# Projection weights stored partition by partition, cache copies cut into 8 KB pieces and partly placed later

## The chip, the cores and the metric

One Trainium2 chip, one of its cores. The metric is the device time of one launch in microseconds (us), lower is better.

## What is computed

One inference step of a one-layer decoder, for a prompt of 1024 tokens and for 8 sample sequences of 4 new tokens (1056 token rows, D = 1024), all float32. Cut to what matters here:

```python
q_a, k_a, v_a, u_b, q_c = split(x @ w_in)            # w_in is 1024 x 2048
attn = mix_of_dilated_windows(q_a, k_a, v_a)          # (128,1), (512,4), (2048,16)
pool = multi_pool(u_b); km, vm = split(mem @ w_mem_kv)
memo = mem_attention(q_c, km, vm)
h1 = layer_norm(alpha * x + concat(attn, pool, memo) @ w_o)
y  = layer_norm(alpha * h1 + hier_moe(h1))            # 32 experts
# for the samples, the K/V windows of 2048 rows move on by the 4 new rows:
new_win_k = concat(cache_win_k, k_new)[:, 4:]         # 8 sequences x 2048 rows x 512
new_win_v = concat(cache_win_v, v_new)[:, 4:]
```

The last two lines are pure copying: 2044 of 2048 rows (2 KB each) of 8 sequences, for K and V, go from the input to the output in HBM. That is 67 MB read and 67 MB written, and nothing in the kernel depends on it.

## The kernel before, in words

The stages come one after another: projection, attention (48 units, with the samples' attention worked in between), output projection with the first layer norm and the router ("mix"), 32 experts, second layer norm. Each engine has a program of its own, written out by hand, and semaphores between them.

**Projection.** The 1056 columns of x transposed (`xT`) and the weights lie in SBUF. Each is split into a rounded high part (ACT, L352, through `rounded_part`) and the rest (DVE, L358, through `rest`), and TensorE adds three products. The list `proj` holds 49 output tiles in the order q (tiles 0 to 11, weight block 0), k (12 to 23, block 1), v (24 to 32, block 2), q_c and u (33 to 44, block 3), memory K/V (45 to 48). A weight block is `[128, 8, 512]`, 2 MB, and has two places, `WF[0]` and `WF[1]`. Blocks 0 and 1 are issued by SP at the start; blocks 2 and 3, `w_mem_kv` and `memT` are issued by POOL (L1565 to L1570), each when `proj_done` says that the tiles using its place are evacuated. Tile n goes to PSUM bank n % 8. DVE evacuates the even tiles (L1134), ACT the odd ones (L962). `splits_after` puts the splits of block 2 behind the evacuations of tiles 12 to 19, and those of block 3 behind tiles 24 to 31: a split that waits for its weights holds up all evacuations behind it on ACT and DVE, and with them TensorE, which can be at most eight tiles ahead.

**The copies.** `copies` has 32 entries of 1022 rows (2,093,056 bytes), numbered 0 to 31 here, issued by SP (L521) in `copy_cache`, which waits for the copy two before it: two are in flight. SP issues 24 (`COPIES_FIRST`) during the projection, and then the score tables (L436), the sample biases and the first two ring loads.

**Attention.** The samples' cached keys and values come through a ring of two slots (L536, from `winkT`, `cache_win_v` and so on); load n may be issued only when step n-2 has been executed by TensorE (`s_xp`). SP issues loads 0 and 1, then all small outputs, then the last 8 copies, and only then load 2. PE's sample steps are `x_step`; those named "ss" use `winkT`.

**Mix.** For each chunk c of 128 rows SP loads `x` (L581, two buffers) and stores `h1` three chunks later (L576).

Of the kernel before, what the change touches and what calls it, by code (L numbers as in the profile page):

```python
# [22 lines left out]
P = 128  # L23
D = 1024
KT = D // P
SEQ = 1024
DB, DT = 8, 4
# [6 lines left out]
N_MEM = 256  # L34
WB = 2048
PB = 15
# [15 lines left out]
NVT = NK // P  # L52

ARENA = 51984
COPIES_FIRST = 24

CAP = 112
LN_SPLIT = 128
# [56 lines left out]
def build(nc, I, O):  # L115
    ctx = ExitStack()
    with ctx:
# [55 lines left out]
        XF, WF = at(18576, KT, TOK), [at(35472 + 8192 * s, KT, 512) for s in range(2)]  # L173
        MT = at(39568, KT, N_MEM)
# [60 lines left out]
        s_xk = [sem(f"s_xk{k}") for k in range(KT)]  # L235
        s_w = [sem(f"s_w{g}") for g in range(5)]
        s_mem, s_state = sem("s_mem"), sem("s_state")
# [46 lines left out]
        def rows(c):  # L284
            return P if c < CH - 1 else SMP
# [214 lines left out]
        @block.sync  # L500
        def _(sp):
            xv = I["xT"].rearrange("(k p) n -> p k n", p=P)
            wv = I["w_in"].rearrange("(k p) n -> p k n", p=P)
            for k in range(KT):
                sp.dma_start(XF[:, k, :], xv[:, k, :]).then_inc(s_xk[k], 16)
                sp.dma_start(WF[0][:, k, :], wv[:, k, 0:512]).then_inc(s_xk[k], 16)
                if k == 1:
                    sp.dma_start(CS[:, :], I["c_small"]).then_inc(s_const, 16)
            sp.dma_start(WF[1], wv[:, :, 512:1024]).then_inc(s_w[1], 16)
            sp.dma_start(USF[:, :, 0:PB], I["stateT"]).then_inc(s_state, 16)  # L510
            sp.dma_start(WPL2[:, :, :], I["w_pool"].rearrange("(m h) c e -> (h c) m e", h=2)).then_inc(s_state, 16)
            sp.dma_start(PSC, I["pool_scale"]).then_inc(s_state, 16)
# [4 lines left out]
            def copy_cache(n):  # L517
                t, b, r = copies[n]
                if n >= 2:
                    sp.wait_ge(s_copy[n % 2], 16 * (n // 2))  # L520
                sp.dma_start(O["win_" + t + "_s"][b, r * half:(r + 1) * half, :],  # L521
                             I["cache_win_" + t][b, DT + r * half:DT + (r + 1) * half, :]).then_inc(s_copy[n % 2], 16)

            for n in range(COPIES_FIRST):
                copy_cache(n)
            load_table(sp, 0)
            sp.dma_start(SBIAS, I["c_sample"]).then_inc(s_bias, 16)
# [1 line left out]
            for n, e in enumerate(ring_user):  # L529
                if n == 0:  # L530
                    proj_done(sp, n_x - 1)
                if n >= 2:
                    sp.wait_ge(s_xp, xnum[ring_user[n - 2]] + 1)
                dst, srcs = ring_load(n, e)
                for d, s in zip(dst, srcs):
                    sp.dma_start(d, s).then_inc(s_ring[n % 2], 16)  # L536
                if n == 1:
                    load_table(sp, 1)
                if n == 2:
                    load_table(sp, 2)  # L540
                if n == 7:
                    load_table(sp, 3)
                if n == 1:
                    proj_done(sp, NPROJ - 1)
                    sp.dma_start(O["kT"].rearrange("(m p) n -> p m n", p=P), KTT[:, :, 0:SEQ]).then_inc(s_store, 16)
                    sp.dma_start(O["v"].rearrange("(c p) n -> p c n", p=P), V[:, 0:CH - 1, :]).then_inc(s_store, 16)
                    sp.dma_start(O["kmT"].rearrange("(m p) n -> p m n", p=P), KM).then_inc(s_store, 16)  # L547
                    sp.dma_start(O["vm"].rearrange("(m p) n -> p m n", p=P), VM).then_inc(s_store, 16)
                    sp.dma_start(O["uT"].rearrange("(m p) n -> p m n", p=P), UP[:, :, UH + SEQ - PB:UH + SEQ]).then_inc(s_store, 16)
                    sp.wait_ge(s_state, 48)  # L550
                    sp.dma_start(O["poolT_s"], USF[:, :, DT:DT + PB]).then_inc(s_store, 16)
                    for b in range(DB):
                        sp.dma_start(O["win_v_s"][b, WB - DT:WB, :], V[DT * b:DT * b + DT, CH - 1, :]).then_inc(s_store, 16)  # L553
                    sp.wait_ge(s_xe, xnum[("knew",)] + 1)
                    for b in range(DB):
                        sp.dma_start(O["win_k_s"][b, WB - DT:WB, :], KN[DT * b:DT * b + DT, :]).then_inc(s_store, 16)
                    for c in range(COPIES_FIRST, len(copies)):
                        copy_cache(c)

            wo = I["w_o"].rearrange("(k p) n -> p k n", p=P)  # L560
# [17 lines left out]
            for c in range(CH):  # L578
                if c >= 2:
                    sp.wait_ge(s_r, c - 1)  # L580
                sp.dma_start(XR[c % 2][0:rows(c), :], I["x"][c * P:c * P + rows(c), :]).then_inc(s_x[c % 2], 16)  # L581
                if c >= 3:
                    store_h1(c - 3)
            sp.wait_ge(s_mix, CH)
# [974 lines left out]
        def _(pool):  # L1559
            step = Steps(pool, s_pl)  # L1560
            G = nc.gpsimd

            wv = I["w_in"].rearrange("(k p) n -> p k n", p=P)
            proj_done(pool, last_of[0])
            G.dma_start(WF[0], wv[:, :, 1024:1536]).then_inc(s_w[2], 16)  # L1565
            proj_done(pool, last_of[1])
            G.dma_start(WF[1], wv[:, :, 1536:2048]).then_inc(s_w[3], 16)
            proj_done(pool, last_of[2])
            G.dma_start(WF[0], I["w_mem_kv"].rearrange("(k p) n -> p k n", p=P)).then_inc(s_w[4], 16)
            G.dma_start(MT, I["memT"].rearrange("(k p) n -> p k n", p=P)).then_inc(s_mem, 16)  # L1570

            proj_done(pool, n_x - 1)
            pool.wait_ge(s_state, 48)
# [105 lines left out]
def laid_out(i):  # L1679

    a = {n: np.asarray(v) for n, v in i.items()}
    x = np.concatenate([a["x_prompt"].reshape(SEQ, D), a["x_sample"].reshape(SMP, D)])

    wk = a["cache_win_k"][0][:, ROWS].reshape(2, 4, 4, KC, 4, 2, HD)
    wk = wk.transpose(0, 3 - 1, 5, 6, 4, 1, 3).reshape(8, P, 4, 4 * KC)
    mk = a["cache_mem_k"][0].reshape(DB, N_MEM, 2, 2, HD).transpose(3, 4, 2, 0, 1).reshape(P, 2, DB * N_MEM)
    out = {
        "x": x, "xT": x.T, "memT": a["mem_prompt"][0].T, "stateT": a["state_pool"][0].transpose(2, 0, 1).reshape(2, P, DB, PB).transpose(1, 0, 2, 3).reshape(P, 2 * DB, PB),
        "winkT": wk, "memkT": mk,
        "cache_win_k": a["cache_win_k"].reshape(DB, WB, D_A), "cache_win_v": a["cache_win_v"].reshape(DB, WB, D_A),  # L1690
        "cache_mem_v": a["cache_mem_v"].reshape(DB, N_MEM, D_C),
        "w_in": a["w_in"][0], "w_mem_kv": a["w_mem_kv"][0], "w_pool": a["w_pool"][0], "pool_scale": a["pool_scale"][0].reshape(2, P).T,
        "w_o": a["w_o"][0], "w_r": np.concatenate([a["w_r1"][0], a["w_r2"][0].transpose(1, 0, 2).reshape(D, NE)], axis=1),
        "b_r": np.concatenate([a["b_r1"][0], a["b_r2"][0].reshape(NE)]),
        "w_gate": a["w_gate"].reshape(NE, D, DE), "w_up": a["w_up"].reshape(NE, D, DE), "w_down": a["w_down"].reshape(NE, DE, D),
        **{n: a[n][0] for n in ("ln1_g", "ln1_b", "ln2_g", "ln2_b")}, **shape_constants(),
    }
    return {n: np.ascontiguousarray(v) for n, v in out.items()}
# [24 lines left out]
```

## Time and profile before

| | |
|---|---|
| median of 3 runs | 1153.97 us |
| the runs | 1158.05, 1153.97, 1153.77 us |
| span of the profiled execution | 1155.0 us |
| that span less the median | 1.0 us |
| TensorE matmul busy | 935.7 us, 81% |
| DVE, ACT, POOL busy | 372.0, 261.9, 196.7 us |
| DMA queue 1 (issued by SP) | 247.97 MB |
| DMA queue 0 (issued by POOL) | 24.66 MB |
| time to landing of a cache copy, median | 13.3 us (K), 13.0 us (V) |
| chain that ended last | PE 64%, DMA 10%, DVE 10%, unknown queue 6% |

The span is what the profile's page covers, and every time below is counted from its start. The profile gives no other time of that execution; the span is 1.0 us above the median. A matmul busy share is not a share of TensorE's peak. The chain of waits is followed back from the last instruction; what it calls an "unknown queue" is a wait whose end no record explains. Of a DMA, "time to landing" runs from its issue to its completion, so it contains the time behind other transfers.

### The profile page before, as it was taken

The numbers are of one execution on the slowest core, as the hardware profiler recorded it, in microseconds if no ns is written. First come the engines' busy times: TensorE is split into PE (matmuls) and PEld (weight loads), VectorE is DVE, ScalarE is ACT, GpSimd is POOL, SyncE is SP. The second block draws the span as 40 slices with busy tenths as digits, with TensorE's granted clock in tenths as the row PEclk, the third lists the DMA queues.
The fourth block names the chain that finished last, engine by engine and source line by source line (L and its number), as shares of the span: only waits on it lengthen the run. The fifth ranks groups of instructions, "written<-read, shape, count | busy, mean of one in ns | idle before, by whom it ended". The sixth has DMA issues, their size and how long they took to land.

```text
span 1155.0 us, 16340 instructions
## 1 busy us (share of the span) xinstructions
PE 935.7 (81%) x6468; PEld 734.8 (64%) x6468; DVE 372.0 (32%) x788; ACT 261.9 (23%) x553; POOL 196.7 (17%) x260
## 2 busy tenths in 40 slices
PE   6993199996868999988999539999999999999100
PEld 6992187993545555557887338878787877878000
DVE  5200202006643556483544460010010101010496
ACT  5100101002433344382222101111111111111121
POOL 0000000042111222250000001212121212211276
PEclk9997599998988999998999758999999999999655
DMA  8999995338997747513221776999898999981461
GB/s 312 340 344 325 342 350 186 110 143 246 306 319 305 252 153 257 186 67 98 74 84 49 261 235 202 326 307 323 291 315 297 324 309 331 313 294 34 173 227 59
DMA packets 118458, 273.43 MB, mean 237 GB/s; under 512 B 13984, under 2 KB 82080, under 8 KB 116224
## 3 DMA queue, kind: packets, MB, share of 16 engines
q1 hardware_dynamic: 108352, 247.97, 63.2%
q0 software_dynamic: 10048, 24.66, 6.2%
q8 instruction: 40, 0.66, 0.2%
q14 instruction: 18, 0.15, 0.0%
HBM read 256.33 MB, written 95.30 MB: 304 GB/s over the span
## 4 chain that ended last, share of the span: by engine, by line
PE 64%; DMA 10%; DVE 10%; another core or an unknown queue 6%; issue 3%; SPq 3%; ACT 2%; POOL 1%; POOLq 0%; DVEq 0%; ACTq 0%
PE psum L641 60%; DMA back<-w_in 4%; DMA out_win_v_s<-cache_win_v 4%; PE psum L700 2%; DVE middle L1221 1%; DMA back<-winkT 1%; DVE front L1456 1%; ACT front L1078 1%; DVE stats L1547 1%; SPq L553 1%; DVE middle L1544 1%; DVE middle L1543 1%; POOL back L1600 1%; SPq L547 1%
## 5 line engine op out<-in xcount | busy, mean ns | idle before, releaser
L641 PE MATMUL psum<-back,front 128*64 128x128 f32 (+2 forms) x1280 | 149.6, 302 | 11.5 <-DVE back L490 7.9
L641 PE MATMUL psum<-x_high,w_high 128*128 128x352 f32 x288 | 95.2, 330 | 54.5 <-DVE w_low L358 54.3
L641 PEld LDWEIGHTS psum<-back,front 128*64 128x64 f32 (+2 forms) x1280 | 108.5, 164 | 45.8 <-issue 30.7
L641 PE MATMUL psum<-back 128*128 128x112 f32 (+3 forms) x1152 | 124.0, 311 | 12.9 <-DMA back<-winkT 10.7
L641 PE MATMUL psum<-front 64*128 64x512 f32 (+5 forms) x448 | 122.1, 514 | 12.1 <-DVE stats L1190 7.4
L641 PEld LDWEIGHTS psum<-back 128*128 128x128 f32 (+1 forms) x1152 | 112.2, 170 | 25.3 <-issue 19.0
L641 PE MATMUL psum<-back,middle 128*128 128x112 f32 (+1 forms) x880 | 101.8, 316 | 1.7 <-issue 1.7
L641 PEld LDWEIGHTS psum<-back,middle 128*128 128x128 f32 (+1 forms) x880 | 91.3, 181 | 14.5 <-issue 14.5
L641 PEld LDWEIGHTS psum<-front 64*128 64x128 f32 (+2 forms) x448 | 52.1, 194 | 67.1 <-issue 48.9
L641 PE MATMUL psum<-x_low,w_high 128*128 128x352 f32 x288 | 94.1, 327 | 0.0
L641 PE MATMUL psum<-x_high,w_low 128*128 128x352 f32 x288 | 94.0, 326 | 0.0
L1600 POOL TENSOR_SCALAR back<-consts,stats 128x128 f32<-128x128 f32 x96 | 57.4, 610 | 199.7 <-DVE stats L1203 141.3
L641 PEld LDWEIGHTS psum<-x_high,w_high 128*128 128x128 f32 x288 | 55.5, 193 | 55.2 <-DVE w_low L358 55.2
L1456 DVE TENSOR_TENSOR front<-front,psum 128x224 f32<-128x224 f32 x32 | 12.4, 388 | 225.5 <-ACT front L1078 225.5
L1461 DVE TENSOR_SCALAR front<-psum,back 112x512 f32<-112x512 f32 x32 | 24.0, 751 | 126.4 <-PE psum L641 126.4
L1620 POOL COPY back<-back 128x1 uint32 (+1 forms) x64 | 12.1, 188 | 303.3 <-DVE front L1461 258.7
L641 PE MATMUL psum<-wo_high,cat_high 128*128 128x512 f32 (+1 forms) x144 | 58.2, 404 | 3.8 <-DVE cat_low L1331 3.8
L700 PE MATMUL psum<-consts,back 128*128 128x128 f32 x352 | 60.2, 290 | 0.1
L1078 ACT ACTIVATE front<-psum 128x224 f32<-128x224 f32 x32 | 11.4, 357 | 205.6 <-PE psum L641 205.6
L358 DVE TENSOR_TENSOR w_low<-back,w_high 128x1024 fp32r<-128x1024 f32 (+1 forms) x20 | 19.8, 1004 | 117.7 <-ACT w_high L352 117.7
L641 PE MATMUL psum<-wo_high,cat_low 128*128 128x512 f32 (+1 forms) x144 | 57.3, 398 | 0.0
L641 PE MATMUL psum<-wo_low,cat_high 128*128 128x512 f32 (+1 forms) x144 | 57.1, 397 | 0.0
(189 smaller groups left out, 1294.6 us busy)
## 6 DMA issues: line engine op xcount, KB each, us to landing
out_win_k_s<-cache_win_k SPq DMA_DIRECT2D x16, 2044.0 KB, 13.3
out_win_v_s<-cache_win_v SPq DMA_DIRECT2D x16, 2044.0 KB, 13.0
front<-w_down SPq DMA_DIRECT2D x16, 1024.0 KB, 7.2
middle<-w_gate SPq DMA_DIRECT2D x16, 1024.0 KB, 5.7
back<-w_up SPq DMA_DIRECT2D x16, 1024.0 KB, 8.1
back<-winkT SPq DMA_DIRECT2D x8, 1792.0 KB, 9.1
back<-cache_win_v SPq DMA_DIRECT2D x8, 1024.0 KB, 7.3
front<-w_gate SPq DMA_DIRECT2D x8, 1024.0 KB, 5.6
```

Of the source, the lines that this page charges most:

```text
L358: nc.vector.tensor_tensor(low, full, high.bitcast(F32), ALU.subtract).then_inc(s_lo, 1)
L547: sp.dma_start(O["kmT"].rearrange("(m p) n -> p m n", p=P), KM).then_inc(s_store, 16)
L553: sp.dma_start(O["win_v_s"][b, WB - DT:WB, :], V[DT * b:DT * b + DT, CH - 1, :]).then_inc(s_store, 16)
L641: return nc.tensor.matmul(out, lhsT, rhs, start=start, stop=stop, skip_group_check=True)
L700: last = nc.tensor.transpose(b[:, (2 * j + s) * P:(2 * j + s) * P + P], SP[(u % 3) * 2 + s][:, kb * P:kb * P + P], ident)
L1078: nc.scalar.activation(SIL[j % 2][:, :, 0:CAP], bank(2 + j % 2)[:, 0:256].rearrange("p (a n) -> p a n", a=2)[:, :, 0:CAP], ACT.Silu).then_ ...
L1221: V_.tensor_tensor(r, r, GB2[0:rows(c), 1, 0:LN_SPLIT], ALU.add).then_inc(s_fo, 1)
L1456: V_.tensor_tensor(AT[j % 2][:, :, 0:CAP], SIL[j % 2][:, :, 0:CAP], bank(2 + j % 2)[:, 256:512].rearrange("p (a n) -> p a n", a=2)[:, :, 0 ...
L1461: V_.tensor_scalar(YS[j % 2][0:CAP, 512:1024], PS[0:CAP, 2048 + 1024 * (j % 2) + 512:2048 + 1024 * (j % 2) + 1024], GS[0:CAP, bass.ds(e, 1 ...
L1543: step(V_.scalar_tensor_tensor(r, H1[0:m, c, :], ALPHA, YP[c % 3][0:m, 0, :], ALU.mult, ALU.add))
L1600: last = G.tensor_scalar(DG[u % 2][:, s, :], ident, RD[:, 2 * u + s:2 * u + s + 1], None, ALU.mult)
L1620: G.tensor_copy(dst, src).then_inc(s_col, 1)
```

## The change

Four host-side arrays get another layout: `w_in` becomes [block, partition, k, 512], `w_mem_kv` and `memT` [partition, k, n], so that what one partition receives of a block (16 KB; 8 KB for `memT`) is contiguous in HBM. `xT` and the k-slices of block 0 keep runs of 4224 bytes and 2 KB. `copy_cache` passes `max_dma_last_dim` = 8176. SP issues 22 copies in the projection, 5 behind the small outputs and one beside each of the first five `x` loads of the mix.

```diff
--- before.py
+++ after.py
@@ -52,7 +52,8 @@
 NVT = NK // P
 
 ARENA = 51984
-COPIES_FIRST = 24
+COPIES_PROJ, COPIES_RING = 22, 5
+COPY_RUN = 2044 * 4
 
 CAP = 112
 LN_SPLIT = 128
@@ -500,13 +501,13 @@
         @block.sync
         def _(sp):
             xv = I["xT"].rearrange("(k p) n -> p k n", p=P)
-            wv = I["w_in"].rearrange("(k p) n -> p k n", p=P)
+            wv = I["w_in"]
             for k in range(KT):
                 sp.dma_start(XF[:, k, :], xv[:, k, :]).then_inc(s_xk[k], 16)
-                sp.dma_start(WF[0][:, k, :], wv[:, k, 0:512]).then_inc(s_xk[k], 16)
+                sp.dma_start(WF[0][:, k, :], wv[0][:, k, :]).then_inc(s_xk[k], 16)
                 if k == 1:
                     sp.dma_start(CS[:, :], I["c_small"]).then_inc(s_const, 16)
-            sp.dma_start(WF[1], wv[:, :, 512:1024]).then_inc(s_w[1], 16)
+            sp.dma_start(WF[1], wv[1]).then_inc(s_w[1], 16)
             sp.dma_start(USF[:, :, 0:PB], I["stateT"]).then_inc(s_state, 16)
             sp.dma_start(WPL2[:, :, :], I["w_pool"].rearrange("(m h) c e -> (h c) m e", h=2)).then_inc(s_state, 16)
             sp.dma_start(PSC, I["pool_scale"]).then_inc(s_state, 16)
@@ -519,9 +520,10 @@
                 if n >= 2:
                     sp.wait_ge(s_copy[n % 2], 16 * (n // 2))
                 sp.dma_start(O["win_" + t + "_s"][b, r * half:(r + 1) * half, :],
-                             I["cache_win_" + t][b, DT + r * half:DT + (r + 1) * half, :]).then_inc(s_copy[n % 2], 16)
-
-            for n in range(COPIES_FIRST):
+                             I["cache_win_" + t][b, DT + r * half:DT + (r + 1) * half, :],
+                             max_dma_last_dim=COPY_RUN).then_inc(s_copy[n % 2], 16)
+
+            for n in range(COPIES_PROJ):
                 copy_cache(n)
             load_table(sp, 0)
             sp.dma_start(SBIAS, I["c_sample"]).then_inc(s_bias, 16)
@@ -554,7 +556,7 @@
                     sp.wait_ge(s_xe, xnum[("knew",)] + 1)
                     for b in range(DB):
                         sp.dma_start(O["win_k_s"][b, WB - DT:WB, :], KN[DT * b:DT * b + DT, :]).then_inc(s_store, 16)
-                    for c in range(COPIES_FIRST, len(copies)):
+                    for c in range(COPIES_PROJ, COPIES_PROJ + COPIES_RING):
                         copy_cache(c)
 
             wo = I["w_o"].rearrange("(k p) n -> p k n", p=P)
@@ -579,6 +581,8 @@
                 if c >= 2:
                     sp.wait_ge(s_r, c - 1)
                 sp.dma_start(XR[c % 2][0:rows(c), :], I["x"][c * P:c * P + rows(c), :]).then_inc(s_x[c % 2], 16)
+                if COPIES_PROJ + COPIES_RING + c < len(copies):
+                    copy_cache(COPIES_PROJ + COPIES_RING + c)
                 if c >= 3:
                     store_h1(c - 3)
             sp.wait_ge(s_mix, CH)
@@ -1560,14 +1564,14 @@
             step = Steps(pool, s_pl)
             G = nc.gpsimd
 
-            wv = I["w_in"].rearrange("(k p) n -> p k n", p=P)
+            wv = I["w_in"]
             proj_done(pool, last_of[0])
-            G.dma_start(WF[0], wv[:, :, 1024:1536]).then_inc(s_w[2], 16)
+            G.dma_start(WF[0], wv[2]).then_inc(s_w[2], 16)
             proj_done(pool, last_of[1])
-            G.dma_start(WF[1], wv[:, :, 1536:2048]).then_inc(s_w[3], 16)
+            G.dma_start(WF[1], wv[3]).then_inc(s_w[3], 16)
             proj_done(pool, last_of[2])
-            G.dma_start(WF[0], I["w_mem_kv"].rearrange("(k p) n -> p k n", p=P)).then_inc(s_w[4], 16)
-            G.dma_start(MT, I["memT"].rearrange("(k p) n -> p k n", p=P)).then_inc(s_mem, 16)
+            G.dma_start(WF[0], I["w_mem_kv"]).then_inc(s_w[4], 16)
+            G.dma_start(MT, I["memT"]).then_inc(s_mem, 16)
 
             proj_done(pool, n_x - 1)
             pool.wait_ge(s_state, 48)
@@ -1685,11 +1689,12 @@
     wk = wk.transpose(0, 3 - 1, 5, 6, 4, 1, 3).reshape(8, P, 4, 4 * KC)
     mk = a["cache_mem_k"][0].reshape(DB, N_MEM, 2, 2, HD).transpose(3, 4, 2, 0, 1).reshape(P, 2, DB * N_MEM)
     out = {
-        "x": x, "xT": x.T, "memT": a["mem_prompt"][0].T, "stateT": a["state_pool"][0].transpose(2, 0, 1).reshape(2, P, DB, PB).transpose(1, 0, 2, 3).reshape(P, 2 * DB, PB),
+        "x": x, "xT": x.T, "memT": a["mem_prompt"][0].T.reshape(KT, P, N_MEM).transpose(1, 0, 2), "stateT": a["state_pool"][0].transpose(2, 0, 1).reshape(2, P, DB, PB).transpose(1, 0, 2, 3).reshape(P, 2 * DB, PB),
         "winkT": wk, "memkT": mk,
         "cache_win_k": a["cache_win_k"].reshape(DB, WB, D_A), "cache_win_v": a["cache_win_v"].reshape(DB, WB, D_A),
         "cache_mem_v": a["cache_mem_v"].reshape(DB, N_MEM, D_C),
-        "w_in": a["w_in"][0], "w_mem_kv": a["w_mem_kv"][0], "w_pool": a["w_pool"][0], "pool_scale": a["pool_scale"][0].reshape(2, P).T,
+        "w_in": a["w_in"][0].reshape(KT, P, 4, 512).transpose(2, 1, 0, 3),
+        "w_mem_kv": a["w_mem_kv"][0].reshape(KT, P, 512).transpose(1, 0, 2), "w_pool": a["w_pool"][0], "pool_scale": a["pool_scale"][0].reshape(2, P).T,
         "w_o": a["w_o"][0], "w_r": np.concatenate([a["w_r1"][0], a["w_r2"][0].transpose(1, 0, 2).reshape(D, NE)], axis=1),
         "b_r": np.concatenate([a["b_r1"][0], a["b_r2"][0].reshape(NE)]),
         "w_gate": a["w_gate"].reshape(NE, D, DE), "w_up": a["w_up"].reshape(NE, D, DE), "w_down": a["w_down"].reshape(NE, DE, D),
```

On SP, from the start of the copies to the third ring load (`winkT`; `out_win_k_s`, `out_win_v_s` are the copies at 32 or 256 rows, and the writes of the 4 new rows at 4x512). Before:

```order
L521 DMA out_win_k_s<-cache_win_k 32x16352 x16
L521 DMA out_win_v_s<-cache_win_v 32x16352 x8
L436 DMA back<-c_table 128x1024 x2
L527 DMA back<-c_sample 128x960
L536 DMA back<-winkT 128x3584 x2
L553 DMA out_win_v_s<-front 4x512 x8
L556 DMA out_win_k_s<-back 4x512 x8
L521 DMA out_win_v_s<-cache_win_v 32x16352 x8
L536 DMA back<-winkT 128x3584
```

With the change:

```order
L522 DMA out_win_k_s<-cache_win_k 256x2044 x16
L522 DMA out_win_v_s<-cache_win_v 256x2044 x6
L437 DMA back<-c_table 128x1024 x2
L529 DMA back<-c_sample 128x960
L538 DMA back<-winkT 128x3584 x2
L555 DMA out_win_v_s<-front 4x512 x8
L558 DMA out_win_k_s<-back 4x512 x8
L522 DMA out_win_v_s<-cache_win_v 256x2044 x5
L538 DMA back<-winkT 128x3584
```

Each copy is now 256 pieces of 2044 elements (8176 bytes) where it was 32 pieces of 16352 elements (65,408 bytes). Two copies fewer stand ahead of the tables, three fewer ahead of the third ring load.

On SP in the mix, with the change (before, no L521 stands here, and the `x` loads follow each other):

```order
L574 DMA routing<-b_r 128x36
L583 DMA back<-x 128x1024
L522 DMA out_win_v_s<-cache_win_v 256x2044
L583 DMA back<-x 128x1024
L522 DMA out_win_v_s<-cache_win_v 256x2044
L583 DMA back<-x 128x1024
L522 DMA out_win_v_s<-cache_win_v 256x2044
L583 DMA back<-x 128x1024
L522 DMA out_win_v_s<-cache_win_v 256x2044
L578 DMA h_d<-back 128x1024
```

The fifth moved copy follows the fifth `x` load.

On POOL, before, the four loads of the projection:

```order
L1565 DMA back<-w_in 128x8x512
L1567 DMA back<-w_in 128x8x512
L1569 DMA back<-w_mem_kv 128x8x512
L1570 DMA back<-memT 128x8x256
```

and with the change:

```order
L1569 DMA back<-w_in 128x4096
L1571 DMA back<-w_in 128x4096
L1573 DMA back<-w_mem_kv 128x4096
L1574 DMA back<-memT 128x2048
```

They stand in the same places; what was eight runs of a partition is one.

## Rows read from the trace of the kernel before

**Rows 1.** The page, in 40 equal slices of the span: granted TensorE clock and DMA busy share.

```profile
PEclk9997599998988999998999758999999999999655
DMA  8999995338997747513221776999898999981461
```

**Rows 2.** Windows: stretch, length, busy of PE PEld DVE ACT POOL, PEclk, DMA share, GB/s.

```profile
95.50:140.00 44.50, 0.04 (x1) 0.00 (x0) 1.56 (x2) 2.64 (x5) 0.00 (x0) 0.53 1.02 342
140.00:151.00 11.00, 10.80 (x50) 10.77 (x51) 5.32 (x8) 2.91 (x6) 0.00 (x0) 0.73 1.06 351
...
338.90:349.70 10.80, 0.14 (x4) 0.00 (x0) 0.73 (x2) 0.35 (x2) 0.00 (x0) 0.58 0.90 322
```

**Rows 3.** Chain of waits: start us, us, what.

```profile
65.52 71.82 another core or an unknown queue
...
140.20 10.54 PE psum L641 x48
...
334.00 15.62 DMA back<-winkT
```

**Rows 4.** Timeline of ACT: start us, us, instruction, idle before.

```profile
65.06 0.47 ACT L962 ACTIVATE front<-psum 128x352 f32<-128x352 f32 x1 [7.17 <-PE psum L641]
137.36 1.04 ACT L352 CAST w_high<-back 128x1024 fp32r<-128x1024 f32 x1 [71.84 <-DMA back<-w_in]
...
193.32 1.05 ACT L352 CAST w_high<-back 128x1024 fp32r<-128x1024 f32 x1 [30.83 <-DMA back<-w_in]
```

**Rows 5.** Timeline of POOL, its DMA issues in the projection.

```profile
58.56 1.13 POOL L1565 DMA_DIRECT2D back<-w_in  x1 [58.12 <-ACT front L962]
151.80 0.92 POOL L1567 DMA_DIRECT2D back<-w_in  x1 [92.11 <-ACT front L962]
201.76 0.88 POOL L1569 DMA_DIRECT2D back<-w_mem_kv  x1 [49.04 <-DVE front L1134]
```

**Rows 6.** DMA from 57 to 138.5 us: queues, and issues with median us to landing.

```profile
q1 hardware_dynamic: 587, 25.77, 92.6%
q0 software_dynamic: 528, 2.10, 8.4%
...
back<-w_in POOLq DMA_DIRECT2D x1, 2048.0 KB, 78.8
```

**Rows 7.** DMA from 27.8 to 58 us, where the copies run alone.

```profile
DMA packets 426, 9.97 MB, mean 330 GB/s; under 512 B 273, under 2 KB 273, under 8 KB 273
```

**Rows 8.** DMA from 200 to 225 us, where no copy runs.

```profile
back<-w_mem_kv POOLq DMA_DIRECT2D x1, 2048.0 KB, 9.9
```

**Rows 9.** Timeline of PE around the stall of the projection.

```profile
95.06 0.32 PE L641 MATMUL psum<-x_low,w_high 128*128 128x352 f32 x1
95.22 0.32 PE L641 MATMUL psum<-x_high,w_low 128*128 128x352 f32 x1
140.20 0.63 PE L641 MATMUL psum<-x_high,w_high 128*128 128x352 f32 x1 [44.66 <-DVE w_low L358]
```

**Rows 10.** Timeline of SP: first table, and copies of the attention stage (two windows).

```profile
247.59 1.90 SPq L436 DMA_DIRECT2D back<-c_table  x2
...
290.88 43.08 SPq L521 DMA_DIRECT2D out_win_v_s<-cache_win_v  x8
...
313.22 0.51 SPq L521 DMA_DIRECT2D out_win_v_s<-cache_win_v  x1
```

**Rows 11.** Timeline of PE around the third ring load.

```profile
326.03 1.72 PE L641 MATMUL psum<-back 128*32 128x224 f32 x32
327.68 1.56 PE L641 MATMUL psum<-front 64*128 64x512 f32 x8
...
349.75 3.21 PE L641 MATMUL psum<-back 128*32 128x224 f32 x32 [10.72 <-DMA back<-winkT]
352.89 2.60 PE L641 MATMUL psum<-front 64*128 64x512 f32 x8
```

**Rows 12.** DMA from 364 to 376 us: a ring load without copies beside it.

```profile
back<-winkT SPq DMA_DIRECT2D x1, 1792.0 KB, 7.0
```

**Rows 13.** Windows: the output projection and layer norm, 523 to 643 us.

```profile
523.00:643.00 120.00, 119.59 (x594) 96.42 (x594) 53.20 (x74) 26.23 (x38) 0.70 (x1) 0.98 0.22 71
```


## Prediction

> **What bounds the kernel now.** I read the page's slices first. The granted TensorE clock is at full speed nearly everywhere and falls to about half in the fourth and fifth slice, with the DMA engines full beside it [rows 1]: TensorE is starved while data moves. The windows give the hole its size: from 95.5 to 140 us TensorE does nothing, in the next 11 us the clock is 0.73, and a second, smaller hole lies at 338.9 to 349.7 us [rows 2]. The chain of waits runs through both: 71.82 us of an unknown queue, a slow piece of PE, and later 15.62 us of a `winkT` load [rows 3].
>
> Who waits in the first hole is seen on ACT. After tile 13 (65.06 us) its next work is the split of block 2, and it sits idle for 71.84 us until `w_in` has landed at about 137.3 us [rows 4]. DVE waits behind ACT, no tile from 14 on is evacuated, and TensorE, eight tiles ahead, stops before tile 22. POOL had issued the load at 58.56 us [rows 5], so the load took 78.8 us. In that time 25.77 MB went through SP's queue and 2.10 MB through POOL's [rows 6]. The same 2 MB took 9.9 us when no copy ran [rows 8]. So the load waits on the copies, which have two 2 MB transfers queued at all times.
>
> How they share is in the packet counts. POOL's queue shows 528 packets: 16 completion marks and 512 of 4096 bytes. SP's 25.77 MB in pieces of 65,408 bytes are 394 pieces. Every packet of weights thus let 25.77 MB / 512 = 50 KB of copies by. The third block, issued at 151.80 us and split from 193.32 us, took 41.5 us, with fewer copies between its packets [rows 4, 5]. The queues take turns by packet and not by byte; that is what the change touches.
>
> **The copies in 8 KB pieces.** If the turns stay as they were (394 pieces per 512 weight packets, 0.77 each), a packet of 4096 bytes lets 6.3 KB of copies by and weights get 4.1 / 10.4 = 39% of the bytes. Copies alone move 330 GB/s [rows 7], which leaves weights 130 GB/s: 2.1 MB in 16 us instead of 78.8. One full piece per packet gives 33% and 19 us; the bound from below is the undisturbed 9.9 us [rows 8].
>
> What is needed is less than that. TensorE stops only when tile 14 is not evacuated as it reaches tile 22, after its last matmul at 95.22 us [rows 9]. Issued at 58.56 us, the load may land until about 93 us, leaving 2.5 us for one split on each engine: 34 us of allowance against 10 to 19. ACT and DVE still wait some 15 us, but TensorE has its eight tiles meanwhile and they catch up. So 44.66 us of idle PE [rows 9] go. The clock goes with it: the 48 matmuls of tiles 22 and 23 take 10.54 us after the hole [rows 3], while matmuls start 0.16 us apart before it [rows 9], which makes 7.7. Another 2.9 us. **Projection: -47.5 us.**
>
> **The weight layout.** The weights of a partition become one run. If a POOL packet stays 4 KB, this does nothing; if it grows to 16 KB, the weights get 16.4 / (16.4 + 6.3) = 72% and land in about 10 us. Both are inside the allowance, so this edit is costed at nothing, and its cover is those 34 us. The Trainium skill, "DMA: Bandwidth & Descriptors", section "SWDGE vs HWDGE vs iDMA", says that such a packet preferably holds at most 4096 bytes, and "Queues, rings and completion order" that an engine goes round robin between rows at packet granularity. Taken strictly, one 64 KB piece per packet would make the old load (65.4 + 4.1) KB x 32 / 20.6 GB/s = 108 us; the trace has 78.8 and 41.5 for it, so turns are not strictly one to one, and for the new load the rule gives the 19 us.
>
> **Block 3, `w_mem_kv`, `memT`.** All are issued 47.5 us earlier, now beside copies. Block 3 may take 41.5 us as before, since TensorE had no hole after 140 us then [rows 1]. The 3.1 MB of the memory loads were issued at 201.76 us [rows 5] and are not wanted before the x part ends, which SP's first table marks at 247.59 us [rows 10]: 46 us, and at 39% they take 24. Nothing waits.
>
> **Do the copies still end in time?** From 27.8 us, 22 copies (46.0 MB) and the POOL loads (7.3 MB) take 53.3 MB / 330 GB/s = 162 us and end at 190 us. The projection's x part now ends at 247.6 - 47.5 = 200 us [rows 10]. That is 10 us of cover, and SP itself is free one copy pair earlier.
>
> **Attention stage.** The second hole is SP's: load 2 of the ring stood behind eight copies, spread from 290.88 over 43.08 us [rows 10], and landed 15.62 us after its issue at 334.00 us [rows 3]. With five copies SP is free after the fifth, which stood at 313.22 us [rows 10]. But load 2 also needs slot 0, which step ss0 frees at 327.7 us [rows 11]. Then the five copies have moved (10.5 MB, 32 us, done at 323 us), and the load needs 7.0 us as one without copies beside it does [rows 12]: it lands at 335. PE came to it at 349.75 - 10.72 = 339.03 us [rows 11], so the 10.72 us of wait go, with 4 us to spare. The clock had fallen to 0.58 [rows 2]; the 32 matmuls took 3.21 us against 1.72 and the eight after them 2.60 against 1.56 [rows 11]: 2.5 us more that go. **Attention: -13.2 us.** Next late would be load 3: it follows ss1 and lands by my reckoning about 1.5 us before its step.
>
> **Copies in the mix.** Each stands behind an `x` load and before the next. DMA is 22% busy there and TensorE has no hole [rows 13]. Two copies and two `x` loads are 5.2 MB, 16 us from 523 us; the third `x` chunk is wanted at 560 us. Later a copy of 6.3 us falls on each 13.7 us chunk. Nothing, while that 22% holds.
>
> **Sum.** -47.5 - 13.2 = -60.7 us: span 1155.0 - 60.7 = 1094.3. The span stood 1.0 above the median, so 1153.97 - 60.7 = **1093.3 us**.
>
> **Rivals.**
> 1. *The second hole stays.* The spare 4 us are thin: tables, small outputs and copies share the queue, and in load 3 there are 1.5 us. If the whole wait stays, only the projection gains: 1106.5. Giving back part of it (DVE and ACT use the hole to catch up) lies between. For it: the attention stage is a chain of many engines. Against: the copies end 5 us before the slot is free. Chance 0.18, the part and the whole together.
> 2. *The share does not change*, because the engines share by bytes or because the smaller piece does not reach the hardware as such. Then block 2 still takes about 79 us and only the attention gains: 1140.8. Against: 512 packets of 4 KB against 394 pieces, and no row shows a share by bytes. Chance 0.04.
> 3. *Slower: short pieces slow the copies themselves.* No row shows HBM to HBM in 8 KB. The copies must end before the tables and ring loads are wanted at 214 us (the attention stage starts some 14 us after the x part). At rate r they end at 27.8 + 53.3 MB / r. It decides below 230 GB/s, where they end at 260 us and eat the 47.5 us gained. At 200 GB/s they end at 294 us; the tables land about 299 us, 85 us late, and the five ring copies (52 us) renew the second wait: 1154 - 47.5 + 85 = 1191. Nearest row: `memT` and `w_mem_kv` in short runs beside nothing, 2.1 MB in 9.9 us with all its latency [rows 8], speaks against a rate so low. The Trainium skill, same page, "How a descriptor splits into AXI transactions", speaks for some loss: a piece that starts off a 256-byte boundary reads one transaction more, and 8176 is 31.9 x 256. By it 33 transactions replace 32, an estimated 3%, and the copies end 5 us later, inside the 10 us. No row shows it. Chance 0.02.
> 4. *More than the sum*, for instance because other loads also leave sooner: down to 1087. Part of the forecast's range.
>
> **How the numbers follow.** Forecast with both holes gone: 0.75, own range 1087 to 1099. Rival 1: 0.18, to 1106.5. Rivals 2 and 3: 0.04 and 0.02, and 0.01 for no change. The range 1087 to 1107 leaves out the last 0.07 and some error of my own sizes. Faster by over 0.5% (about what a measurement of this kernel can tell from no change) are all cases but rival 3 and the last 0.01: 0.97; within 0.5% 0.01; slower 0.02.
>
> **What would show it.** Right: block 2 lands 10 to 20 us after its issue; PE has no idle piece between 10 and 200 us; clock 1.0 there; copies still 300 GB/s or more; tables issued at about 200 us; the third `winkT` load lands within 9 us and PE does not wait for it; PE in the mix as before. Wrong: a load of `w_in` over 34 us; tables issued after 205 us; a wait for `winkT` of several us; chunks of the mix over 13.7 us apart.

## The result, and the profile after

The changed kernel takes 1303.53 us (median of 4 runs, 1301.6 to 1304.9) where the kernel before takes 1154.64 (1153.77 to 1158.05): a ratio of 1.128, 95% interval 1.126 to 1.130. I had forecast 1093.3.

The page of the profile after, in its 40 slices, stands against [rows 1]. The span is 1300.9 us.

```profile
PEclk9999998555558969999989997699999999999855
DMA  8999999999999997746369937579998999994352
GB/s 304 151 193 195 131 220 139 133 136 132 140 290 180 147 172 275 264 170 212 130 139 178 165 109 260 191 266 317 324 303 298 300 327 320 320 312 149 138 201 77
```

The hole of the projection is no longer there, but a larger one has come behind it, over five slices. The DMA engines are as busy as before and move 131 to 220 GB/s instead of 330. The windows say where TensorE stands (columns as in [rows 2]):

```profile
9.00:95.50 86.50, 86.50 (x536) 86.50 (x536) 27.69 (x33) 23.23 (x33) 0.76 (x1) 1.00 0.98 215
95.50:200.00 104.50, 104.50 (x557) 92.86 (x556) 11.81 (x17) 9.45 (x16) 3.12 (x4) 1.00 1.00 178
200.00:214.00 14.00, 12.62 (x62) 10.47 (x60) 1.53 (x3) 0.77 (x2) 11.93 (x8) 1.00 0.96 144
214.00:378.00 164.00, 0.00 (x0) 0.00 (x0) 0.23 (x1) 0.00 (x0) 0.00 (x0) 0.51 0.98 146
```

Through the projection TensorE never idles and its clock is full, as forecast. At 214 us it stops for 164 us. What it waits for is seen on DVE, in its timeline:

```profile
377.77 0.29 DVE L1194 CUSTOM_DVE_ANT_0 back<-psum,back 128x128 f32<-128x128 f32 x1 [164.24 <-DMA back<-c_table]
```

It is the first score table, `c_table`. SP's timeline shows why it is late, against [rows 10] (there the first table was issued at 247.59 us):

```profile
27.97 228.89 SPq L522 DMA_DIRECT2D out_win_k_s<-cache_win_k  x16
272.53 78.00 SPq L522 DMA_DIRECT2D out_win_v_s<-cache_win_v  x6
350.65 1.00 SPq L437 DMA_DIRECT2D back<-c_table  x2
...
403.18 55.00 SPq L522 DMA_DIRECT2D out_win_v_s<-cache_win_v  x5
458.22 0.61 SPq L538 DMA_DIRECT2D back<-winkT  x1
```

The 22 copies keep SP until 350.5 us. The page's DMA issues give the time of one, which was 13.3 and 13.0 us before:

```profile
out_win_k_s<-cache_win_k SPq DMA_DIRECT2D x16, 2044.0 KB, 31.9
out_win_v_s<-cache_win_v SPq DMA_DIRECT2D x16, 2044.0 KB, 31.3
```

From 205 to 330 us, where the copies run alone, the DMA view shows queue 1 busy for 97% of the 16 engines' time and 135 GB/s, against 330 in [rows 7]:

```profile
DMA packets 2198, 16.92 MB, mean 135 GB/s; under 512 B 129, under 2 KB 129, under 8 KB 2197
```

The load of block 2 beside them, from 57 to 100 us, against [rows 6]:

```profile
q1 hardware_dynamic: 726, 5.67, 81.7%
q0 software_dynamic: 144, 2.10, 17.4%
...
back<-w_in POOLq DMA_DIRECT2D x1, 2048.0 KB, 26.4
```

POOL's queue has 144 packets where it had 528: 2.10 MB in 128 packets are 16 KB each, and 16 are completion marks. The second hole of TensorE, at [rows 11] 10.72 us, has grown:

```profile
489.45 3.21 PE L645 MATMUL psum<-back 128*32 128x224 f32 x32 [25.40 <-DMA back<-winkT]
```

**The account, in the two spans.** The projection ends 49.2 us sooner (the first matmul of the attention stage starts at 212.10 us instead of 261.27). The wait for the first table adds 164.8 us (PE is idle for 165.6 us where it was for 0.9), the longer wait for `winkT` 14.7 us, and 9.3 us are the rest of the attention stage. Part of these is a TensorE at the lower clock after the idle time: 0.50, which is 1.2 GHz, from 378 to 385 us, 0.69 to 400 us and 0.81 to 489 us, against 0.96 from 270 to 338 us before. So the mix starts at 663.0 us instead of 523.4: +139.6. It takes 125.6 us instead of 118.8: +6.7. There PE waits 2.0 us for DVE between 740 and 755 us, and its clock is 0.66 in these 15 us. What follows is 0.4 us shorter. Sum +145.9 us, which is 1300.9 - 1155.0.

### The profile page after: what moved, and what is told of

Same layout as the page of the kernel before. It is cut to its first block, busy times and chain, and to the rows that moved or that the text cites. A ratio compares the mean times of both kernels' runs of the same rounds, so it can differ in the third digit from the quotient of the medians.

```text
span 1300.9 us, 16340 instructions
## 1 busy us (share of the span) xinstructions
PE 942.9 (72%) x6468; PEld 738.7 (57%) x6468; DVE 372.5 (29%) x788; ACT 262.2 (20%) x553; POOL 195.2 (15%) x260
## 4 chain that ended last, share of the span: by engine, by line
PE 46%; DMA 32%; DVE 9%; SPq 6%; issue 3%; ACT 2%; POOL 1%; POOLq 0%; DVEq 0%; ACTq 0%
PE psum L645 43%; DMA out_win_k_s<-cache_win_k 20%; DMA out_win_v_s<-cache_win_v 9%; DMA back<-winkT 2%; PE psum L704 2%; DVE middle L1225 1%; SPq L512 1%; SPq L549 1%; DVE front L1460 1%; ACT front L1082 1%; SPq L548 1%; DVE stats L1551 1%; DVE middle L1548 1%; DVE middle L1547 1%; POOL back L1604 1%
## 5 line engine op out<-in xcount | busy, mean ns | idle before, releaser
L645 PE MATMUL psum<-front 64*128 64x512 f32 (+5 forms) x448 | 126.4, 531 | 176.6 <-DVE stats L1194 171.9
L645 PEld LDWEIGHTS psum<-front 64*128 64x128 f32 (+2 forms) x448 | 54.8, 204 | 232.9 <-DVE stats L1194 177.7
L1194 DVE CUSTOM_DVE_ANT_0 back<-psum,back 128x128 f32<-128x128 f32 (+7 forms) x64 | 47.6, 746 | 172.4 <-DMA back<-c_table 164.2
L984 ACT ACTIVATE back<-back,stats 128x128 f32<-128x128 f32 (+7 forms) x64 | 49.7, 777 | 174.3 <-DVE stats L1194 174.3
L704 PE MATMUL psum<-consts,back 128*128 128x128 f32 x352 | 60.7, 292 | 0.1
## 6 DMA issues: line engine op xcount, KB each, us to landing
out_win_k_s<-cache_win_k SPq DMA_DIRECT2D x16, 2044.0 KB, 31.9
```

The source lines that it names most:

```text
L645: return nc.tensor.matmul(out, lhsT, rhs, start=start, stop=stop, skip_group_check=True)
L704: last = nc.tensor.transpose(b[:, (2 * j + s) * P:(2 * j + s) * P + P], SP[(u % 3) * 2 + s][:, kb * P:kb * P + P], ident)
L984: nc.scalar.activation(sp[:, 0:w], src, ACT.Exp, scale=-1.0, bias=MN[:, x:x + 1], accum_out=DEN[:, x:x + 1]).then_inc(s_exp, 1)
L1194: V_.tensor_tensor_reduce(SP[(u % 3) * 2 + s][:, 0:w], ps[:, 0:w], TB[hp % 2][s][:, SEQ - w:SEQ], 1.0, 3e38, ALU.add, ALU.min, MN[:, x:x + ...
```

## The experiments

All but e4 are the changed kernel with one thing different. e3, e4, e5 and h3 do all of the work and ran four times; their ratio to the kernel before, run on the same chip, is given with its interval. The others ran once each, beside the kernel before at 1150.2 to 1151.9 us, and leave out 3 to 6% of the copied bytes, as their texts say. The four runs of h3 lie up to 4.4 us apart, so differences of a few us between single runs are not read here; the slow cases stand out by over 140 us.

### Taking the change apart

**e3, long pieces, all else kept.**

```diff
-                             I["cache_win_" + t][b, DT + r * half:DT + (r + 1) * half, :],
-                             max_dma_last_dim=COPY_RUN).then_inc(s_copy[n % 2], 16)
+                             I["cache_win_" + t][b, DT + r * half:DT + (r + 1) * half, :]).then_inc(s_copy[n % 2], 16)
```

> The change without its 8 KB pieces: weight layout and the 22/5/5 placing kept, copies in 65,408-byte pieces as before. The trace after shows POOL's packets of weights grown to 16 KB (128 per block where there were 512). If each packet lets 50 KB of copies by as before, block 2 lands in (2.1 + 6.4) MB / 330 GB/s = 26 us, inside the 34 us of allowance, both holes of TensorE go and the time is 1093 us. With one to one turns of 64 KB it is 32 us, still inside. Rival (shares go by bytes, 8% as before): 79 us again, and about 1141 us.

1095.42 us (1095.14 to 1095.59), against 1150.23 of the kernel before: ratio 0.952 (0.950 to 0.954). The DMA view of 56 to 100 us:

```profile
q1 hardware_dynamic: 305, 13.61, 85.4%
q0 software_dynamic: 144, 2.10, 13.3%
...
back<-w_in POOLq DMA_DIRECT2D x1, 2048.0 KB, 26.9
```

and its windows:

```profile
9.00:95.50 86.50, 86.50 (x533) 86.50 (x532) 27.69 (x33) 23.38 (x33) 0.76 (x1) 1.00 0.99 349
95.50:200.00 104.50, 104.50 (x557) 92.94 (x556) 11.81 (x17) 9.45 (x16) 2.45 (x4) 1.00 0.80 288
```

The load takes 26.9 us, where 26 were computed from 50 KB of copies per packet, and TensorE has no hole in the projection. In its timeline step ss2, the third one that uses `winkT`, follows without a wait:

```profile
288.17 1.72 PE L644 MATMUL psum<-back 128*32 128x224 f32 x32
```

So the whole loss is in the 8176-byte pieces: 208 us between 1303.5 and 1095.4, of which some 4 are the difference between the kernel before beside the one (1154.64) and beside the other (1150.23). And larger weight packets do without short pieces what I had expected of these.

**e4, weight layout alone** (e3 with the placing of before):

```diff
-COPIES_PROJ, COPIES_RING = 22, 5
+COPIES_PROJ, COPIES_RING = 24, 8
```

> The kernel before with the weight layout alone: long pieces, 24 copies in the projection and 8 behind the small outputs. If larger weight packets are what shortens the load, the first hole (47.5 us) goes and the second (13.2 us) stays: 1106 to 1107 us. If shares go by bytes: 1154 us, no change.

1103.56 us (1103.02 to 1106.81), ratio 0.960 (0.958 to 0.962): the layout is worth 46.7 us and the placing another 8.1. That larger packets make the load itself quicker can't be it: in the old layout it took 9.9 us when no copy ran [rows 8], so nearly all of the 78.8 us was waiting. The second hole is still there, but shorter:

```profile
295.93 3.22 PE L644 MATMUL psum<-back 128*32 128x224 f32 x32 [3.80 <-DMA back<-winkT]
```

### What makes 8176-byte pieces slow

The measure in all of these is the median time to landing of a K copy of 2 MB: 13.3 us before, 31.9 with the change. The two first theories were the uneven start and the size.

**e1, pieces of 8192 bytes at multiples of 8192** (the edit in part: `...` marks what is left out, and `COPY_RUN` is 2048 * 4):

```diff
-                sp.dma_start(O["win_" + t + "_s"][b, r * half:(r + 1) * half, :], ...
+                e0, np_ = r * 256 * 2048, 256 - 16 * r
+                dst = O["win_" + t + "_s"][b].rearrange("r n -> (r n)")[e0:e0 + np_ * 2048]
+                sp.dma_start(dst.rearrange("(p n) -> p n", n=2048), ...
```

> The changed kernel with copies in pieces of 8192 bytes that start at multiples of 8192, where the change has 8176 bytes at multiples of 8176 (16-byte boundaries). Left out of the computation: the last 15 pieces (120 KB) of each sequence's K and V copy, 3% of the copied bytes. Theory ALIGN (it is the uneven start of the pieces that made the copies fall from 330 to 135 GB/s): the copies run at about 330 GB/s again, the tables are issued at about 200 us, and the time is about 1093 us. Theory SIZE (each piece has a fixed price of its own: 8176 bytes took 0.97 us on one of 16 DMA engines and 65,408 bytes 3.17 us, which is 0.66 us plus 38 ns per KB): still 135 to 140 GB/s, tables at about 345 us, time about 1300 us (1290 with the 3% left out).

12.2 us, 1095.30 us in all. SIZE falls. Its block 2 of the weights lands in 14.9 us:

```profile
out_win_k_s<-cache_win_k SPq DMA_DIRECT2D x8, 2048.0 KB, 12.2
...
back<-w_in POOLq DMA_DIRECT2D x1, 2048.0 KB, 14.9
```

**e2, the same 16 bytes further on** (`e0 = 4 + ...`):

> As the run before, with every piece of the copies moved by 16 bytes, so that size and number are the same and only the alignment is that of the change. Left out: the same 3% and the first 16 bytes. ALIGN: 135 GB/s and about 1295 us, some 200 us over the aligned one. SIZE: the same as the aligned one within 1%.

14.1 us, 1097.84. That is 2.5 us over e1, no more than the same kernel can differ from run to run, and not 200. ALIGN falls too; both my theories were wrong. Some loss there may be: from 28 to 56 us the DMA engines moved 295 GB/s, in e1 322. The V copies took 13.2 us against 12.2.

**f1, 8176 bytes at multiples of 8192** (`[:, 0:2044]` of rows of 2048 elements):

> Pieces of 8192 bytes were fast at either offset, so neither ALIGN nor SIZE stands; what is left of the difference is the odd length (8176 = 16 x 511 bytes) or that pieces start at ever changing offsets (multiples of 8176). Here every piece is 8176 bytes and starts at a multiple of 8192. Left out: the last 16 bytes of each piece and the last 15 pieces of each sequence. Theory LENGTH: copies at about 135 GB/s, 1290 to 1300 us. Theory START: 320 GB/s or more, about 1095 us.

13.0 us, 1097.05.

**f2, 8192 bytes at multiples of 8208** (rows of 2052 elements):

> The counterpart: every piece is 8192 bytes and starts at a multiple of 8208, so that starts change by 16 bytes from piece to piece. Left out: 16 bytes between pieces and the last pieces of each sequence. LENGTH: 320 GB/s or more, about 1095 us. START: about 135 GB/s, 1290 to 1300 us.

26.7 us, 1244.93: the slowness is back, so the length is not it, and the places of the pieces are. The DMA issues of f2:

```profile
out_win_k_s<-cache_win_k SPq DMA_DIRECT2D x8, 2048.0 KB, 26.7
```

**f3 and f4, contiguous pieces of 8160 and 8128 bytes:**

> Contiguous pieces of 8160 bytes (32 x 255), the last 15 of each sequence and the remainder left out. If the slow case needs a length or start that is no multiple of 32 bytes, this is fast (about 1095 us). If the border is 64 bytes or more, it is as slow as the change (135 to 140 GB/s, about 1290 us).

> Contiguous pieces of 8128 bytes (64 x 127), left out as before. Fast (about 1095 us) if multiples of 64 bytes are enough; slow, 135 to 140 GB/s, if the length must be a multiple of 128 bytes or more (the pieces of the kernel before, 65,408 = 128 x 511, would fit that too).

12.8 us and 1097.67; 12.6 us and 1100.44. Steps of 32 or 64 bytes are harmless. That left starts that differ by odd multiples of 16 bytes, and four runs were made on how they mix.

**g1, one alignment per engine; g2, pairs at 0 and 16; g3, source side alone; g4, destination side alone.** The access patterns of the first half of a sequence, as [step, count] in elements of 4 bytes (worked out from the edits, not lines of them):

```text
[[2044, 256], [1, 2044]]                the change
[[32772, 16], [2048, 16], [1, 2048]]    g1, both sides
[[4112, 128], [2052, 2], [1, 2048]]     g2, both sides; g3 source, g4 destination
```

In g3 and g4 the other side has a step of 2048 between the two pieces of a pair.

> What made the copies slow is where the pieces start: lengths of 8176, 8160, 8128 and 8192 bytes are fast when all starts of a copy agree modulo 32 bytes (all at 0, or all at 16), and slow when starts at 0 and at 16 modulo 32 occur in one copy. Theory MIX: it is the mixture within what one DMA engine works through. Theory ODD: any piece that starts at 16 modulo 32 is slow unless something else holds. Here a copy has 16 rows of 16 (or 14) contiguous pieces of 8192 bytes, row after row 16 bytes further on, so that by the outer dimension one engine gets one row and keeps one alignment, while engines differ. Left out: 16 bytes after each row and the end of each sequence. MIX: fast, 300 GB/s or more, about 1096 us. If the mixture between engines is enough: about 150 to 170 GB/s and 1240 us or more.

> Pairs of 8192-byte pieces at a stride of 16,448 bytes (a multiple of 64): the even piece starts at 0, the odd one at 16 modulo 64, on both sides. Left out: the gaps and the end of each sequence. MIX: slow, about 150 to 170 GB/s and 1240 us or more, although only two alignments occur. If more variety is needed (in the change all four multiples of 16 modulo 64 occur, further on all modulo 256): fast, about 1096 us.

> As the pairs before, but only the source piece is moved by 16 bytes; all destination pieces start at multiples of 64. The output is therefore shifted in every other piece, and the gaps are left out. If reads are the slow side: as slow as the pairs with both sides moved. If writes are: about 1096 us.

> The other way round: only the destination piece is moved by 16 bytes, the sources start at multiples of 64. Output shifted in every other piece, gaps left out. If writes are the slow side: as slow as the pairs with both sides moved. If reads are: about 1096 us.

13.7, 12.9, 12.5 and 12.7 us; 1097.53, 1099.76, 1095.67 and 1099.21 us in all. None is slow, MIX falls, and with no slow case the two sides can't be told apart. What was left was where the 16 engines stand. If each takes 16 pieces in a row, they work 130,816 bytes apart with pieces of 8176 and 131,328 with a stride of 8208, each 256 bytes off 131,072.

**h1, rows 130,816 bytes apart, aligned pieces; h2, rows 131,072 apart, contiguous 8176-byte pieces** (patterns as above):

```text
[[2044, 256], [1, 2044]]                the change
[[32704, 16], [2048, 15], [1, 2048]]    h1
[[32768, 16], [2044, 16], [1, 2044]]    h2
[[32704, 16], [2044, 15], [1, 2044]]    k1, further down
```

> Two alignments in one copy did not slow it, so MIX falls. The slow copies (pieces at multiples of 8176 and of 8208) have two things left that no fast one has: starts that run through all multiples of 16 bytes, and engines that start 256 bytes less or more than 131,072 apart (16 x 8176 = 130,816; 16 x 8208 = 131,328), if an engine gets 16 pieces in a row. Here a copy is 16 rows 130,816 bytes apart, each of 15 contiguous pieces of 8192 bytes, so that all starts are multiples of 64. Left out: the end of each row, 6% of the bytes. Theory STARTS (the running offset of 16 bytes is the cause): fast, about 1095 us. Theory SPACING (the distance between the places where the engines work at the same time is the cause): slow, 135 to 170 GB/s, 1240 us or more.

> The counterpart: 16 (or 15) rows 131,072 bytes apart, each of 16 pieces of 8176 bytes that follow each other without a gap, as in the change; only the rows are 256 bytes further apart than there. Left out: 256 bytes of each row and the end of each sequence. STARTS: slow, 135 to 170 GB/s, 1240 us or more. SPACING: fast, about 1096 us.

The DMA issues of h1:

```profile
out_win_k_s<-cache_win_k SPq DMA_DIRECT2D x16, 1920.0 KB, 12.0
```

and of h2:

```profile
out_win_k_s<-cache_win_k SPq DMA_DIRECT2D x8, 2044.0 KB, 14.4
```

1095.23 and 1096.92 us. Both fast: neither property alone is enough.

No view names the engine that took a packet, so that an engine takes one row, or 16 pieces in a row, is my reading. One figure fits it: the second copy of a sequence has 15 rows in h2, and queue 1 of h2 has 114,352 packets where f1, with as many pieces in one dimension, has 114,368. That is one completion mark less for each of these 16 copies, as if 15 engines had worked.

**k1, both together in 16 rows; k2, 256 pieces in one dimension at a stride of 8240:**

> Distance of 130,816 bytes alone was fast, and running starts in rows 131,072 bytes apart were fast. Here both stand together: 16 rows 130,816 bytes apart, each of 15 contiguous pieces of 8176 bytes. That is the change less every sixteenth piece, but written as 16 rows, so that one engine gets one row. Left out: those pieces, 6% of the bytes. Theory BOTH (it takes the running starts and the distance of 131,072 less 256 together): slow, 135 to 170 GB/s, 1240 us or more. Theory FORM (it takes the running starts and the copy written as one dimension of 256 pieces, which may be dealt to the engines another way): fast, about 1096 us.

> One dimension of 256 (or 240) pieces of 8192 bytes, at a stride of 8240 bytes: starts run through all multiples of 16 modulo 64, by 48 each time, and 16 pieces are 131,840 bytes. Left out: the gaps and the end of each sequence. FORM: slow, 135 to 170 GB/s, 1240 us or more. BOTH: fast, about 1097 us.

The DMA issues of k1:

```profile
out_win_k_s<-cache_win_k SPq DMA_DIRECT2D x16, 1916.2 KB, 35.7
```

and of k2:

```profile
out_win_k_s<-cache_win_k SPq DMA_DIRECT2D x8, 2048.0 KB, 13.5
```

1375.78 and 1100.23 us. k1 differs from h2 in 256 bytes between rows (and a sixteenth piece less), and from h1 in 16 bytes between pieces, and copies at little more than a third of their speed. With e1 (131,072 and 8192 bytes) these are all four combinations of the two steps, and only one is slow. BOTH holds, FORM falls. k1 has the addresses of the change less every sixteenth piece, and its copies take longer than the change's (35.7 us against 31.9) with fewer bytes; no run says why. Why the two together do it (a resource in HBM or in the DMA engines that such addresses meet in at the same time is my guess) isn't shown by any run, nor what other distances and steps do it (f2 has the signs of both turned, and is slow), nor which side, read or write, is slow.

### The correction

**e5, one number; h3, rows split 1024 and 1020** (both edits in one, h3's in part):

```diff
-COPY_RUN = 2044 * 4
+COPY_RUN = 4088 * 4                     # e5
+COPY_RUN = 2048 * 4                     # h3
+                r0, r1 = (0, 1024) if r == 0 else (1024, WB - DT)   # h3
```

> The change with one number different: pieces of 16,352 bytes (128 per copy) instead of 8176. Starts are multiples of 32; engines are still 130,816 bytes apart. Nothing is left out. STARTS: fast, 1095 us. SPACING: the copies are slow again, 1200 us or more.

> The whole change with short pieces that start at multiples of 32: each sequence is split into 1024 and 1020 rows, which gives 256 pieces of 8192 and 256 of 8160 bytes. Nothing is left out. Both lengths were fast alone. About 1095 us; the weight loads land about 15 us after their issue instead of 27, which was inside the allowance anyway, so the same as with long pieces within 0.2%.

1096.36 us (1094.85 to 1097.27), ratio 0.951 (0.948 to 0.954), and 1096.98 us (1095.74 to 1100.13), ratio 0.951 (0.948 to 0.954). Both, and e3, do all of the work at 0.951 to 0.952 of the kernel before; no run tells them apart. e5 has the distance of 130,816 bytes (8 pieces) with starts at multiples of 32 and is fast. Beside h1 and the kernel before (two pieces of 65,408 are 130,816 bytes too) that is a third witness that the distance alone is harmless.

## Why the prediction was wrong

**The step that failed** is "Do the copies still end in time?", where 53.3 MB were divided by the 330 GB/s of [rows 7]. That row is a rate of 65,408-byte pieces, and I let it stand for 8176-byte pieces. They ran at 135 GB/s alone, and all traffic from 28 to 350 us came to 158 GB/s, with which the same sum has the copies end at 365 us and not at 190. Of the 10 us of cover nothing was left: SP issued the tables at 350.65 us instead of about 200, and TensorE waited 164 us for them.

**Rival 3 was the right mechanism**, with its place (the tables behind the copies, the `winkT` wait renewed) and its border of 230 GB/s. It was priced at 200 GB/s and given 0.02. The row held against it, 2.1 MB in 9.9 us [rows 8], is HBM to SBUF, and says nothing of HBM to HBM; I wrote that no row shows it and then used one. The Trainium skill, "DMA: Bandwidth & Descriptors", section "How a descriptor splits into AXI transactions", starts the first transaction of a piece that is not aligned at the 256-byte boundary below it, and from that I had estimated 3%. For a constant offset e2 had 295 GB/s against 322 in e1, some 8% in single runs, and no loss that the kernel's time shows. The factor 2.4 of the change is nothing that rule gives: most of the fast patterns of the table below start off such a boundary too.

**The projection: right in time, by another edit than the one that had the credit.** Forecast -47.5 us; the projection ended 49.2 us sooner, and e4 measured -46.7. Block 2 took 26.4 us where I took 16, still inside the allowance of 34; with fast short pieces (e1) it took 14.9.

**The weight layout: costed at nothing, and enough alone.** I took POOL's packet to stay at 4 KB or to matter little, and gave the -47.5 us to the short pieces. The trace has 128 packets of 16 KB instead of 512 of 4 KB. The Trainium skill, "DMA: Bandwidth & Descriptors", section "SWDGE vs HWDGE vs iDMA", says that a packet holds "preferably" at most 4096 bytes; these packets hold 16 KB, and the measurement decides. With long pieces kept, the load took 26.9 us (e3) and the whole gain was there; short pieces on top of the layout gained nothing (h3). Short pieces with the old layout were never run, so what they are worth alone is open.

**The turns: by packet, with a count of their own for each size.** With pieces of 65,408 bytes the turns by packet are borne out: 4 times fewer packets shorten the load from 78.8 to 26.9 us. For short pieces I kept 0.77 pieces per weight packet, and e1 shows otherwise. From the issue of its block 2 at 57.85 us to 62.2 us POOL's queue has no packet; from 62.5 to 72.2 us the DMA view has

```profile
q0 software_dynamic: 139, 2.03, 52.9%
q1 hardware_dynamic: 209, 1.59, 43.5%
```

2.03 MB are 124 packets of 16 KB, and 1.59 MB are 194 pieces of 8192 bytes: 1.6 per packet. In e3, from 63.0 to 84.8 us, 6.28 MB beside 2.06 MB are 96 pieces and 126 packets, 0.8 each. So in e1 the weights got 56% of the bytes and not 72%, and my sum had nothing for the 4 us and more before the first packet. If a packet of 4096 bytes let 1.6 such pieces by, an estimate for short pieces with the old layout is 24% of the 350 GB/s that all queues moved in [rows 2], 25 us, and 4 or 5 us ahead of it: about 30 us where the prediction had 16, against the allowance of 34. The forecast of the projection would then still hold, with little room; no run shows it. What brought the 47 us here was the layout.

**The attention: right in kind, 13.2 forecast, 8.1 measured** (e4 to e3). In e3 no wait for `winkT` is left, as computed. But in e4 the hole to be removed was 3.80 us, no longer 10.72, since the third ring load was issued some 5 us sooner, counted from the end of the projection, than before. The term was sized on a hole that the first term had already made smaller.

**The mix: right but for the rate.** 119.4 us in e3, with the same five copies there, against 118.8. With the change it is 6.7 us longer, the 2.0 us of waiting and the low clock after it; e3 has neither, so the slow copies are what brought them.

**The sum** was -60.7 us. e3 gives -54.8 us in medians on one chip, and -61.4 in the spans of the two profiles; the profile of before spans 1155.0 us, where the same kernel on the chip of e3 had a median of 1150.23. What was forecast for the change holds for the change without its piece size.

## What to carry to other kernels

When an urgent load shares the DMA engines with bulk copies, look at the size of its own packets first: here a host-side layout gave 46.7 of the 54.8 us and touched nothing else, and smaller pieces of the bulk added nothing to it. How many pieces of the bulk go by per packet has to be counted again when their size changes: it went from 0.8 to 1.6. A rate in a trace belongs to its pattern; one for pieces of another size, stride or kind of memory has to be measured before a queue's worth of work is planned with 10 us of cover. And a piece length is a choice of addresses too: 16,352 and 8160 bytes were as good as 8192, and 8176 lost over 200 us.

## What the runs showed that I had not expected

Copies HBM to HBM, two in flight:

| pattern (bytes) | time of a K copy of 1.96 to 2.1 MB, us | kernel, us |
|---|---|---|
| 65,408 contiguous (before) | 13.3 | 1154.0 |
| 8176 contiguous (the change) | 31.9 | 1303.5 |
| 16 rows 130,816 apart, of 15 contiguous 8176 (k1) | 35.7 | 1375.8 |
| 8192 at stride 8208 (f2) | 26.7 | 1244.9 |
| 16 rows 131,072 apart, of 16 contiguous 8176 (h2) | 14.4 | 1096.9 |
| 16 rows 130,816 apart, of 15 contiguous 8192 (h1) | 12.0 | 1095.2 |
| 8192 contiguous (e1) | 12.2 | 1095.3 |
| the same, 16 further on (e2) | 14.1 | 1097.8 |
| 16 rows 131,088 apart, of 16 contiguous 8192 (g1) | 13.7 | 1097.5 |
| pairs of 8192 at 0 and 8208, next pair at 16,448 (g2) | 12.9 | 1099.8 |
| 8192 at stride 8240 (k2) | 13.5 | 1100.2 |
| 8176 at stride 8192 (f1) | 13.0 | 1097.1 |
| 8160 contiguous (f3) | 12.8 | 1097.7 |
| 8128 contiguous (f4) | 12.6 | 1100.4 |
| 16,352 contiguous (e5) | 13.9 | 1096.4 |
| 8192 and 8160 contiguous (h3) | 12.9 and 13.6 | 1097.0 |

Slow are only those where each piece starts 16 bytes less or more than 8192 after the last, and sixteen pieces, by my reading the share of one engine, start 256 bytes less or more than 131,072 after the sixteen before. And a POOL packet of a plain load held a whole contiguous run of 16 KB.
